# Routing and expert loop of a hybrid decoder layer: expert 0 first and loaded during routing, down projection one block behind, its weights on GpSimd's queue

## The chip, the cores and the metric

The kernel runs on one core of a Trainium2 chip. The metric is device time in microseconds for one launch of the whole layer; the median of several runs is compared.

## The reference, cut to what matters

One decoder layer over 2048 tokens of width 1024: a parallel pair of attention and state-space heads, an output projection, and then a mixture of experts with 32 experts in 4 groups. Each token goes to the two best experts of its best group. The part that this change touches:

```
g_sel = argmax(h @ w_router_group + b)                 # 1 of 4 groups
top_p, top_i = top_k(softmax(e_logits of that group), 2)
dest: rows sorted by expert, each expert padded to whole blocks of 128 rows
for each block of 128 rows, with its expert e:
    hid = silu(xb @ w_gate[e]) * (xb @ w_up[e])        # 1024 -> 512
    out = hid @ w_down[e]                              # 512 -> 1024
x = x + sum over a token's two rows of gate * out row
```

All inputs and outputs are float32. w_gate, w_up and w_down take 2 MiB for each expert, 6 MiB in all.

## The kernel before, in words

The layer is a chain of stages, each a function with its own semaphores and one or more blocks in which the five engines run their own programs. A stage ends with a barrier over all engines. The three last stages matter here: `route`, `experts`, `combine`.

`route` (lines 1238 to 1404) is one long chain of small VectorE instructions, almost each waiting for the one before it. It finds the two experts of each token, counts rows with two TensorE matmuls (`pref_done`), sums the counts in 16 additions into `rank_base` (line 1365), compares them with block edges (1367), reduces to blocks for each expert (1369), makes a prefix sum (1370) and a difference (1371), and writes the tables `slot_ids` (the 128 token numbers of each block) and `block_meta` (for each block the place of its expert among the experts that have rows; then their numbers, and the count of blocks and experts). ScalarE computes three exponentials here, GpSimd prepares a few constants at the start, and SyncE has nothing to do.

`experts` (lines 1407 to 1620) has two blocks. The first only sets buffers and semaphores (VectorE memsets) and stores one block of zeros. In the second each engine loops over the filled blocks of 128 rows, of which there are 49 for this input; the number is known only at run time.

- SyncE loads gate, up and down weights of expert after expert, each 2 MiB in one transfer into one buffer (`w_gate_raw` and so on). It waits until the earlier expert's weights in that buffer have been split.
- Every float32 matmul is done in three passes over values split into a high part (float32r) and a low part. ScalarE makes the high part of weights by a copy (`split_hi`, line 1488), VectorE the low part by subtraction (`split_lo`, line 1533), each in halves of 128x2048. The split weights have one buffer only, so a new expert's weights can be split only when TensorE has finished with the old ones. All splits stand under a test that the next block's expert differs (`where_below`).
- GpSimd gathers the rows of the next block with an indirect DMA, after TensorE has transposed the rows of the block before.
- TensorE does for block b: gate (24 matmuls, line 1576 on), up (24), the first half of the transposes of the rows of block b+1 (`rows_T(0)`, line 1569), the transposes of the hidden values (line 1603), `rows_T(1)`, and down (24 matmuls, lines 1614 to 1619).

The hidden values of block b are `silu(gate) * up`. So between the last up matmul and the transposes stands a VectorE multiplication (line 1551), and between the transposes and the first down matmul a ScalarE copy (line 1510):

```
                    product(U, 1, u_done)
                    pe.wait_ge(x_in, 16 * b + 32)
                    rows_T(0)
                    pe.wait_ge(hid_done, b + 2)
                    ...
                    rows_T(1)
                    pe.wait_ge(hh_done, b + 2)
```

`combine` gathers each token's two result rows, adds them and makes the final norm. It isn't touched.

## Time and profile before

| | us |
|---|---|
| median of 3 runs | 2601.83 |
| lowest and highest | 2600.53, 2602.84 |
| the profiled execution's own time | 2598.93 |
| its span in the profile | 2597.2 |
| `route`, about | 1464.8 to 1508 |
| `experts`, up to TensorE's first weight matmul | 1509.3 to 1542.6 |
| `experts`, block loop, about | 1542.6 to 2502 |
| `combine`, about | 2506 to 2597 |

Times within the profile are microseconds from the start of the span. PE is TensorE, PEld its weight loads, DVE is VectorE, ACT is ScalarE, POOL is GpSimd, SP is SyncE. A TensorE matmul's duration in the rows reaches over the start of the next one, so the distance between two starts is the better measure of its cost.

### The profile page before, as it was taken

The numbers are of one execution on the slowest core, as the hardware profiler recorded it, in microseconds if no ns is written. First come the engines' busy times: TensorE is split into PE (matmuls) and PEld (weight loads), VectorE is DVE, ScalarE is ACT, GpSimd is POOL, SyncE is SP. The second block draws the span as 40 slices with busy tenths as digits, with TensorE's granted clock in tenths as the row PEclk, the third lists the DMA queues.
The fourth block names the chain that finished last, engine by engine and source line by source line (L and its number), as shares of the span: only waits on it lengthen the run. The fifth ranks groups of instructions, "written<-read, shape, count | busy, mean of one in ns | idle before, by whom it ended". The sixth has DMA issues, their size and how long they took to land. (4 is left out here: it accounts for less than half of the span.)

```text
span 2597.2 us, 29608 instructions
## 1 busy us (share of the span) xinstructions
PE 2193.0 (84%) x9806; PEld 1650.3 (64%) x9807; DVE 1421.5 (55%) x2441; ACT 1110.1 (43%) x1586; POOL 276.6 (11%) x348
## 2 busy tenths in 40 slices
PE   4999999948969687876999549999999999999950
PEld 3764444448447576765888437777777777777740
DVE  4831582045258576674544557566648847354548
ACT  6101111012317576665222126566647847355432
POOL 0002331024220110000000000000000000000022
PEclk6999999979869898998999759999999999999985
DMA  7023443172742514311433158477758958454649
GB/s 223 33 73 138 170 142 118 41 245 112 314 112 69 114 27 88 86 29 51 134 128 134 51 218 347 186 282 279 279 210 340 370 227 333 168 198 195 253 172 378
DMA packets 128019, 458.76 MB, mean 177 GB/s; under 512 B 25136, under 2 KB 41536, under 8 KB 113600
## 3 DMA queue, kind: packets, MB, share of 16 engines
q1 hardware_dynamic: 98352, 345.22, 38.0%
q0 software_dynamic: 18928, 69.49, 7.1%
q10 hardware_dynamic: 10656, 43.00, 4.0%
q8 instruction: 46, 0.75, 0.1%
q14 instruction: 37, 0.30, 0.0%
HBM read 342.06 MB, written 115.61 MB: 176 GB/s over the span
## 5 line engine op out<-in xcount | busy, mean ns | idle before, releaser
L1533 DVE TENSOR_TENSOR w_gate_lo<-w_gate_raw,w_gate_hi 128x2048 fp32r<-128x2048 f32 x64 | 146.3, 2286 | 179.0 <-ACT w_gate_hi L1488 179.0
L895 DVE CUSTOM_DVE_ANT_0 scores<-c_bank,alibi 128x512 f32<-128x512 f32 (+3 forms) x320 | 175.4, 607 | 109.0 <-PE c_bank L993 108.8
L488 PE MATMUL a_bank<-w_in_chunk,hT 128*128 128x512 f32 x512 | 221.9, 596 | 0.7 <-ACT hT L266 0.7
L488 PE MATMUL a_bank<-hT,w_in_chunk 128*128 128x512 f32 x512 | 220.6, 593 | 0.0
L300 ACT ACTIVATE proj_out<-a_bank 128x512 f32<-128x512 f32 x64 | 38.2, 597 | 398.7 <-PE a_bank L488 389.4
L488 PEld LDWEIGHTS a_bank<-w_in_chunk,hT 128*128 128x128 f32 x512 | 128.8, 252 | 92.7 <-issue 62.6
L1007 PE MATMUL c_bank<-v_head,map_T 128*128 128x128 f32 x1088 | 152.2, 289 | 41.7 <-ACT map_T L951 41.7
L1576 PE MATMUL m_bank<-w_gate_hi,rows_T_hi 128*128 128x512 f32 x392 | 154.9, 395 | 24.2 <-DVE rows_T_lo L1537 24.2
L1614 PE MATMUL m_bank<-w_down_hi,hidden_T_hi 128*128 128x512 f32 x392 | 160.4, 409 | 16.2 <-ACT hidden_T_hi L1510 16.2
L488 PEld LDWEIGHTS a_bank<-hT,w_in_chunk 128*128 128x128 f32 x512 | 97.0, 190 | 120.9 <-issue 120.8
L1007 PEld LDWEIGHTS c_bank<-v_head,map_T 128*128 128x128 f32 x1088 | 136.2, 198 | 57.4 <-ACT map_T L951 57.4
L992 PE MATMUL c_bank<-k_hi,q_parts 128*128 128x512 f32 (+3 forms) x320 | 126.9, 401 | 43.9 <-DMA k_lo<-kT_d 37.8
L940 ACT ACTIVATE scores<-scores,neg_max 128x128 f32<-128x128 f32 (+15 forms) x128 | 152.6, 1199 | 19.6 <-DVE neg_max L900 19.5
L1578 PE MATMUL m_bank<-w_gate_hi,rows_T_lo 128*128 128x512 f32 x392 | 157.1, 401 | 0.0
L1578 PE MATMUL m_bank<-w_up_hi,rows_T_lo 128*128 128x512 f32 x392 | 156.1, 398 | 0.0
L1577 PE MATMUL m_bank<-w_gate_lo,rows_T_hi 128*128 128x512 f32 x392 | 155.4, 397 | 0.0
L1615 PE MATMUL m_bank<-w_down_lo,hidden_T_hi 128*128 128x512 f32 x392 | 155.2, 396 | 0.0
L1577 PE MATMUL m_bank<-w_up_lo,rows_T_hi 128*128 128x512 f32 x392 | 154.5, 394 | 0.0
L1576 PE MATMUL m_bank<-w_up_hi,rows_T_hi 128*128 128x512 f32 x392 | 153.8, 392 | 0.0
L1533 DVE TENSOR_TENSOR w_up_lo<-w_up_raw,w_up_hi 128x2048 fp32r<-128x2048 f32 x64 | 143.5, 2283 | 1.7 <-ACT w_up_hi L1488 1.7
L1488 ACT ACTIVATE w_gate_hi<-w_gate_raw 128x2048 fp32r<-128x2048 f32 x64 | 122.3, 1912 | 51.5 <-DMA w_gate_raw<-in_w_gate_dram 51.1
L1533 DVE TENSOR_TENSOR w_down_lo<-w_down_raw,w_down_hi 128x2048 fp32r<-128x2048 f32 x64 | 143.4, 2282 | 0.4 <-ACT w_down_hi L1488 0.4
(375 smaller groups left out, 4427.0 us busy)
## 6 DMA issues: line engine op xcount, KB each, us to landing
w_gate_raw<-in_w_gate_dram SPq DMA_DIRECT2D x32, 2048.0 KB, 7.8
w_up_raw<-in_w_up_dram SPq DMA_DIRECT2D x32, 2048.0 KB, 10.7
w_down_raw<-in_w_down_dram SPq DMA_DIRECT2D x32, 2048.0 KB, 10.7
rows_d<-rows_out ACTq DMA_DIRECT2D x50, 512.0 KB, 10.3
rows_d<-zero_rows POOLq DMA_DIRECT2D x34, 512.0 KB, 18.6
x_tile<-in_x_dram SPq DMA_DIRECT2D x16, 512.0 KB, 3.8
w_in_chunk<-in_w_in_dram POOLq DMA_DIRECT2D x4, 2048.0 KB, 14.9
qT_d<-xn_tile SPq DMA_DIRECT2D x32, 256.0 KB, 3.1
```

The costliest lines, as they stand in the source:

```text
L488: last = pe.matmul(bank[4 + n % PB][:], lhsT, rhs, start=kt == 0, stop=kt == KT - 1)
L895: dve.tensor_tensor_reduce(S[:, s, m, c * BANK:c * BANK + w], bank[n % 4][:, 0:w], bias[:, h % 2, x0:x0 + w], 1.0, -BIG, ALU.add, ALU.max, ...
L940: act.activation(S[:, s, m, 0:L], S[:, s, m, 0:L], ACT.Exp, bias=nm[:, s, m:m + 1], accum_out=rs[:, s, m:m + 1]).then_inc(exped, 1)
L992: pe.matmul(bank[n % 4][:, 0:w], qt, kh[:, m, cols].bitcast(F32R), start=True, stop=False)
L1007: last = pe.matmul(bank[6 + u % 2][:, 0:VD], aT[:, n % 2, b * P:(b + 1) * P], v[:, h % 2, kt], start=kt == 0, stop=kt == u % NT)
L1488: act.activation(whi[w][:, s], raw[w][:, s], ACT.Copy).then_inc(hi_done[w], 1)
L1533: dve.tensor_tensor(wlo[w][:, s], raw[w][:, s], whi[w][:, s], ALU.subtract).then_inc(lo_done[w], 1)
L1576: pe.matmul(to[:], xh[:, k], whi[w][:, c], start=k == 0, stop=False)
L1577: pe.matmul(to[:], xh[:, k], wlo[w][:, c], start=False, stop=False)
L1578: last = pe.matmul(to[:], xl[:, k], whi[w][:, c], start=False, stop=k == KT - 1)
L1614: pe.matmul(DN[h][:], hh[:, k], whi[2][:, part(k)], start=k == 0, stop=False)
L1615: pe.matmul(DN[h][:], hh[:, k], wlo[2][:, part(k)], start=False, stop=False)
```

## The change

In `route`: the weight buffers and their semaphores are made before the stage (class `ExpertStore`). SyncE starts the loads of expert 0's gate and up weights at the start of the stage, GpSimd those of its down weights. ScalarE splits off all six high halves. The low halves: VectorE makes the first of gate, in its chain after the gates are computed and ahead of the wait for `pref_done`; GpSimd makes the second of gate and both of up; the two of down are made by VectorE at the start of `experts`. Expert 0 gets at least one block, so that it is always first. GpSimd makes the zero block and sets three semaphores, ScalarE stores the zeros. The first block of `experts` goes away.

In `experts`: the loop runs over blocks but one. TensorE's order in iteration j is gate of block j+1, transposes of the hidden values of block j, up of block j+1, both halves of the row transposes of block j+2, down of block j. Loads are in halves of 1 MiB, each issued when its half of the buffer has been split; the down halves are issued by GpSimd after its gather. ScalarE copies out both halves of the result, of which VectorE made one before, and loads the table with Silu once before the loop.

```
-def route(nc, ident, ones, logits, gates, dest, ids, meta, d):
+def route(nc, ident, ones, logits, gates, dest, ids, meta, store, a, d):
...
+            def split_lo(eng, w, i):
+                eng.wait_ge(hi_done[w], i + 1)
+                return eng.tensor_tensor(wlo[w][:, halves[i]], raw[w][:, halves[i]], whi[w][:, halves[i]], ALU.subtract)
+
+            @block.sync
+            def _(sp):
+                for w in range(2):
+                    for i in range(2):
+                        sp.dma_start(raw[w][:, halves[i]], store.source(a, w, slice(0, 1), i)).then_inc(w_in[w][i], 16)
...
+                for i in range(2):
+                    pool.dma_start(raw[2][:, halves[i]], store.source(a, 2, slice(0, 1), i)).then_inc(w_in[2][i], 16)
+                pool.memset(store.out[:], 0.0).then_inc(primed, 1)
...
+                pool.wait_ge(lo_done[0], 1)
+                split_lo(pool, 0, 1).then_inc(lo_done[0], 1)
+                split_lo(pool, 1, 0).then_inc(lo_done[1], 1)
+                split_lo(pool, 1, 1).then_inc(lo_done[1], 1)
...
                 act.activation(gex[:], gex[:], ACT.Exp).then_inc(exp_done, 1)
+                act.wait_ge(primed, 1)
+                act.dma_start(d["rows"][NBLK], store.out[:]).then_inc(store.out_st, 16)
+                split_hi(0, 0)
                 act.wait_ge(exp_in, 3)
...
+                split_hi(0, 1)
+                for w in range(1, 3):
+                    for i in range(2):
+                        split_hi(w, i)
+                act.wait_ge(store.out_st, 16)
...
+                split_lo(dve, 0, 0).then_inc(lo_done[0], 1)
                 dve.wait_ge(pref_done, 1)
...
+                step(dve.tensor_scalar(nblk[:, 0:1], nblk[:, 0:1], 1.0, None, ALU.max))
...
+                step(dve.tensor_scalar(bf[0:1, META_LATER:META], pend[0:1, NE - 1:NE], -1.0, None, ALU.add))
...
 (experts, SyncE)
+                with sp.Fori(1, n) as o:
+                    e = expert(sp, o)
+                    for w in range(2):
+                        for i in range(2):
+                            sp.wait_ge(lo_done[w], 2 * o - 1 + i)
+                            load(sp, w, e, i)
 (GpSimd)
+                with pool.Fori(2, n) as b:
+                    past, now = place(pool, b - 2), place(pool, b - 1)
+                    e = expert(pool, now + 1)
+                    pool.wait_ge(xT_psum, 2 * b + 2)
+                    gather(b + 1)
+                    with where_below(nc, pool, past, now):
+                        for i in range(2):
+                            pool.wait_ge(lo_done[2], 2 * now + 1 + i)
+                            load(pool, 2, e, i)
 (ScalarE)
+                act.preload_act_table(ACT.Silu)
...
+                with act.Fori(0, later(act)) as j:
+                    before, now, order = place(act, j), place(act, j + 1), place(act, j + 2)
+                    hidden_hi(j + 1)
+                    act.wait_ge(g_done, j + 2)
+                    act.wait_ge(hid_done, j + 1)
                     act.activation(sil[:], G[:], ACT.Silu).then_inc(silu_done, 1)
                     with where_below(nc, act, now, order):
+                        split_hi(0, order, 0)
+                        split_hi(0, order, 1)
+                    rows_hi(0, 2 * j + 5)
+                    rows_hi(1, 2 * j + 6)
                     with where_below(nc, act, now, order):
+                        act.wait_ge(u_done, j + 2)
+                        split_hi(1, order, 0)
+                    out_half(0, j)
                     with where_below(nc, act, now, order):
+                        split_hi(1, order, 1)
+                    out_half(1, j)
+                    store(j)
+                    with where_below(nc, act, before, now):
+                        split_hi(2, now, 0)
+                        split_hi(2, now, 1)
 (VectorE)
+                with dve.Fori(0, later(dve)) as j:
+                    before, now, order = place(dve, j), place(dve, j + 1), place(dve, j + 2)
+                    hidden_lo(j + 2)
                     with where_below(nc, dve, now, order):
+                        split_lo(0, order, 0)
+                        split_lo(0, order, 1)
+                    hidden(j + 1)
+                    rows_lo(0, 2 * j + 5)
+                    rows_lo(1, 2 * j + 6)
                     with where_below(nc, dve, now, order):
+                        split_lo(1, order, 0)
+                        split_lo(1, order, 1)
+                    with where_below(nc, dve, before, now):
+                        split_lo(2, now, 0)
+                        split_lo(2, now, 1)
 (TensorE: gate and up of block 0 and the row transposes of block 1 stand ahead of the loop)
+                with pe.Fori(0, later(pe)) as j:
+                    before, order = place(pe, j), place(pe, j + 1)
...
+                    product(G, 0, g_done)
+                    hidden_T(j)
...
+                    product(U, 1, u_done)
+                    pe.wait_ge(x_in, 16 * j + 48)
+                    rows_T(0)
+                    rows_T(1)
+                    down(j, before)
+                end = later(pe)
+                hidden_T(end)
+                down(end, place(pe, end))
```

`store.source(a, w, e, i)` is the half i of weight w of expert e in memory, laid out as before. `down` waits for both down halves (`hi_done[2]`, `lo_done[2]`) and for `d_used`, both copies of the result before.

## Rows read from the trace of the kernel before

**Rows 1.** The page's head, and its part on DMA issues.

```profile
span 2597.2 us, 29608 instructions
...
w_gate_raw<-in_w_gate_dram SPq DMA_DIRECT2D x32, 2048.0 KB, 7.8
...
w_in_chunk<-in_w_in_dram POOLq DMA_DIRECT2D x4, 2048.0 KB, 14.9
```

**Rows 2.** Windows view: busy us of each engine (instructions), granted clock, DMA share, GB/s.

```profile
1510.50:1542.50 32.00, 1.97 (x8) 1.57 (x8) 14.68 (x8) 12.10 (x8) 2.62 (x5) 0.50 0.93 372
1542.50:2500.00 957.50, 918.12 (x4109) 738.18 (x4110) 568.52 (x430) 576.01 (x511) 64.60 (x144) 1.00 0.65 252
1563.10:1621.60 58.50, 56.11 (x253) 45.12 (x253) 44.71 (x31) 40.47 (x35) 4.04 (x9) 1.00 0.95 370
2537.00:2547.00 10.00, 0.00 (x0) 0.00 (x0) 9.29 (x12) 2.48 (x6) 4.10 (x4) 0.50 1.03 417
```

**Rows 3.** Waits in the block loop: us in total, times, longest.

```profile
ACT w_gate_hi L1488 <- DMA w_gate_raw<-in_w_gate_dram: 2.1, 1, 2.1
PE m_bank L1603 <- DVE hidden L1551: 22.6, 48, 2.3
PE m_bank L1614 <- ACT hidden_T_hi L1510: 15.8, 47, 0.5
```

**Rows 4.** Timeline of one block in the loop, TensorE: start, us, what.

```profile
2001.63 0.40 PE L1576 MATMUL m_bank<-w_up_hi,rows_T_hi 128*128 128x512 f32 x1
...
2007.24 0.60 PE L1569 MATMUL m_bank<-ident,rows_in 128*128 128x128 f32 x4
...
2008.27 0.75 PE L1603 MATMUL m_bank<-ident,hidden 128*128 128x128 f32 x4 [0.43 <-DVE hidden L1551]
...
2008.85 0.61 PE L1569 MATMUL m_bank<-ident,rows_in 128*128 128x128 f32 x4
...
2009.85 0.50 PE L1614 MATMUL m_bank<-w_down_hi,hidden_T_hi 128*128 128x512 f32 x1 [0.39 <-ACT hidden_T_hi L1510]
...
2015.55 0.39 PE L1576 MATMUL m_bank<-w_gate_hi,rows_T_hi 128*128 128x512 f32 x1
```

**Rows 5.** Timeline of the start of the expert stage, all engines.

```profile
1509.29 0.91 DVE L1444 MEMSET rows_out<- 128x1024 f32 x1 [1.24 <-PEq L62]
...
1511.06 0.18 POOL L1473 COPY idx<-slot_ids 128x1 int32<-128x1 int32 x1 [44.88 <-POOLq L1440]
...
1516.43 1.97 PE L1569 MATMUL m_bank<-ident,rows_in 128*128 128x128 f32 x8 [9.33 <-DMA rows_in<-h_d,idx]
...
1523.48 3.71 ACT L1488 ACTIVATE w_gate_hi<-w_gate_raw 128x2048 fp32r<-128x2048 f32 x2 [49.05 <-DMA w_gate_raw<-in_w_gate_dram]
1525.43 4.49 DVE L1533 TENSOR_TENSOR w_gate_lo<-w_gate_raw,w_gate_hi 128x2048 fp32r<-128x2048 f32 x2 [15.01 <-ACT w_gate_hi L1488]
...
1540.89 1.28 DVE L1537 TENSOR_TENSOR rows_T_lo<-m_bank,rows_T_hi 128x512 fp32r<-128x512 f32 x2
...
1542.63 0.76 PE L1576 MATMUL m_bank<-w_gate_hi,rows_T_hi 128*128 128x512 f32 x1 [24.22 <-DVE rows_T_lo L1537]
```

**Rows 6.** Timeline of VectorE within the routing.

```profile
1479.93 0.09 DVE L1363 MEMSET rank_base<- 128x32 f32 x1 [2.74 <-PE r_bank L1301]
...
1483.59 0.69 DVE L1367 TENSOR_TENSOR compare<-rank_base,block_edges 128x512 f32<-128x512 f32 x1
```

**Rows 7.** Timeline of an earlier stage: VectorE beside GpSimd, and alone.

```profile
558.12 1.25 POOL L552 TENSOR_TENSOR sin_z<-z_state,table_batch 128x510 f32<-128x510 f32 x1
558.35 1.57 DVE L573 TENSOR_TENSOR z_in<-z_in,z_tmp 128x512 f32<-128x512 f32 x1
...
565.53 0.69 DVE L573 TENSOR_TENSOR z_in<-z_in,z_tmp 128x512 f32<-128x512 f32 x1
```

**Rows 8.** Groups by line in the block loop, ScalarE: busy us, mean ns.

```profile
L1505 ACT ACT_TABLE_LOAD x49 | 62.9, 1283 | 37.4 <-issue 36.9
...
L1505 ACT ACTIVATE silu<-m_bank 128x512 f32<-128x512 f32 x49 | 29.4, 600 | 1.3 <-PE m_bank L1578 0.8
```

More of the change, by code:

```diff
@@ L1460, in _, with load @@
+            def load(eng, w, e, i):
+                eng.dma_start(raw[w][:, halves[i]], store.source(a, w, bass.ds(e, 1), i)).then_inc(w_in[w][i], 16)
             @block.sync
@@ L1496, in _, with store @@
+                def store(b):
+                    act.wait_ge(d_used, 2 * b + 4)
+                    act.dma_start(d["rows"][bass.ds(b, 1)].rearrange("o p n -> p (o n)"), out[:]).then_inc(out_st, 16)
+                act.preload_act_table(ACT.Silu)
                 rows_hi(0, 1)
                 rows_hi(1, 2)
-                with act.Fori(0, blocks(act)) as b:
-                    now, order = place(act, b), place(act, b + 1)
-                    with where_below(nc, act, now, order):
-                        act.wait_ge(g_done, b + 1)
-                        split_hi(0, order, (0,))
-                    act.wait_ge(g_done, b + 1)
-                    act.wait_ge(hid_done, b + 1)
+                first, second = place(act, 0), place(act, 1)
@@ L1542, in _ @@
+                split_lo(2, 0, 0)
                 rows_lo(0, 1)
                 rows_lo(1, 2)
[L1544 to L1563 removed]
@@ L1565, in _ @@
+                end = later(dve)
+                hidden_lo(end + 2)
             @block.tensor
```

254 lines of the change are left out of this document (136 added, 118 removed).

## The prediction, made before the changed kernel was run

> **What bounds the kernel now.** I read the page first [rows 1], then the windows view, to see which engine fills each stretch [rows 2]. In the block loop TensorE is busy 918.1 of 957.5 us at the full clock of 2.4 GHz (1.00), while VectorE has 568.5, ScalarE 576.0 and the DMA engines a share of 0.65. So TensorE sets the loop, and all that can be won there is its idle time, 39.4 us, plus what its pipeline loses in refilling after each wait. Ahead of the loop stands the opposite: 32 us in which TensorE does 2 us of work and the DMA engines are 0.93 busy. These 32 us are a load, not arithmetic.
>
> The waits view says what the loop's 39.4 us are [rows 3]: 22.6 us before the transposes of the hidden values, for the VectorE product, and 15.8 us before down, for the ScalarE copy, both about once in every block. The timeline of one block shows them in place [rows 4]: up from 2001.63 to 2007.24, transposes, 0.43 idle, hidden transposes, row transposes, 0.39 idle, down from 2009.85, next gate at 2015.55. The block takes 5.60 (gate, 2015.55 to the next up by the same 24 matmuls) + 5.61 + 2.61 + 5.70, that is 19.5. Up's 24 matmuls take 5.61 and down's 5.70, so a restart costs some 0.1 beyond the idle time shown.
>
> The start of the expert stage [rows 5] shows that the gather index is read at 1511.06, rows are there at 1516.43, but the first weights only at 1523.48, and that splitting the three weights one after the other (ScalarE 3.71, VectorE 4.49 each pair) puts the low part of the rows, queued behind them on VectorE, at 1540.89 and the first matmul at 1542.63.
>
> **Part 1: what `route` takes on.** Loads: 6.29 MB at the 417 GB/s that a full stretch reached [rows 2] take 15 us; from 1465 they end by about 1483. ScalarE's halves of 1.86 each [rows 5] follow and end by about 1488; its exponentials are waited for once, at about 1476, ahead of which only one half stands, loaded first. Cost 0 to 2 us if that half is late; I take 0. VectorE's own low half (4.49 / 2 = 2.25) stands in front of the wait for the counts, where VectorE idled 2.74 [rows 6]: 0, and 2.25 if that wait were shorter. Two added one-value or 32-value instructions of VectorE: about 0.2 each, 0.4 us.
>
> The three low halves on GpSimd are the doubtful part. No GpSimd subtraction of 128x2048 is in the trace. A 128x510 one took 1.25 [rows 7]; four times that is 5.0, and scaled as VectorE's do (0.69 for 512 [rows 7], 2.25 for 2048 [rows 5]) it is 4.1. I take 4.6, so 14 us from about 1479.6 on, done long before the stage's end at 1508. But rows 7 also show that they aren't free for VectorE: its L573, with both inputs in SBUF, takes 0.69 alone and 1.57 when it starts 0.23 after a GpSimd multiplication of 1.25. It ended at 559.92, that is 0.55 after GpSimd's end: it stood still until GpSimd had finished. In `route` VectorE's 16 additions read PSUM and one SBUF tile, and I let them run. Then come, from 1483.59 [rows 6], instructions with two SBUF inputs. Compare stands until GpSimd's first half ends at 84.2: 0.6 lost. During compare's 0.69 GpSimd's second half stands and then runs 84.9 to 89.5. VectorE does the reduction and the maximum, about 0.9, and stands at the prefix sum until 89.5: 3.7 lost. The third half slips in behind it, 89.7 to 94.3, and the difference stands 4.6 less a little. Together 8.7 us (7.3 to 10 with halves of 4.1 to 5.0; 0 if the additions or luck keep the two apart). `route` gets longer by 8.7 + 0.4 = 9.1.
>
> The Trainium skill has this as a rule (SBUF — State Buffer, Who interferes with whom): an exclusive lock, held for a whole instruction, between a GpSimd instruction that reads SBUF and a VectorE one with two SBUF inputs. The trace agrees (1.57 against 0.69). With that rule the route costs the 9.1 above; without it 0.4, which is the second rival.
>
> **Part 2: the start of `experts`.** The first block goes: index at 1511.06 came 1.77 after the point 1509.29 at which the stage's first instruction can start [rows 5]; −1.8. From the index the rows need 5.37 as before, then 1.97 for eight transposes at the lower clock, and 0.6 + 0.65 + 0.45 for high part, low part and TensorE's start, about 9.0, since gate's and up's splits are done and only one half of down (2.25) stands ahead on VectorE while the rows are on their way. Before it was 1542.63 − 1511.06 = 31.6. Gain 22.5. Parts 1 and 2 together: −15.2.
>
> **Part 3: the loop.** In the new order each TensorE step has work between it and what it needs, so I take both waits and the restarts as gone: 39.4 + 48 x 0.1 = 44.2. What covers them, counted from the end of a gate, in a block after which the expert changes (TensorE: hidden transposes to 0.6, up to 6.2, row transposes to 7.4, down to 13.0, gate to 18.6):
> - ScalarE: hidden copy to 1.3, Silu to 1.9, two gate halves to 5.7, two row copies (0.6 each, as Silu [rows 8]) from 7.0 to 8.2, up half to 10.1, result half to 10.9, up half to 12.8, result half to 13.7, store, two down halves to 18.0. It needs six halves and six copies, 15.1 of 18.6.
> - VectorE: hidden low to 2.0, gate lows to 8.4, product to 9.1, row lows to 10.4, up lows to 15.2, down lows to 20.7, ahead of 26.0 where down wants them. It needs 13.5 + 2.7 = 16.2 of 18.6.
> - Next gate at 13.0 wants row lows (10.4) and gate lows (8.4); next up at 19.2 wants 15.2. Nothing is late; the tightest has 2.6 us.
> - Loads: each half of 1 MiB is asked for when its low half is done (6.1 to 20.7) and wanted 14 us later. SyncE has four of them in a block. GpSimd issues the down halves after its gather, and nothing else is queued behind them but the next gather, wanted 5 us later still. If the cover goes, a late load costs its lateness.
>
> The table load of 1.283 ahead of each Silu [rows 8] ought to go, as Silu's table is loaded ahead of the loop and the copies are found under it. If one stays in each block ScalarE needs 16.4, if two 17.7, still below 18.6. The Trainium skill puts the price of a change of table at 1283 ns plus 1380 ns of drain (ScalarE: Activation LUTs, What ACT_TABLE_LOAD costs). The row has the first number. By the sum with drain two loads would make 20.4 and ScalarE the bound; the trace shows no such second part in the block loop, where Silu follows its load directly.
>
> New costs: the first switch has no filled pipeline. Block 0's gate ends 8 us after the first matmul (slow clock for about 5 of it, as before). From there Silu and two gate halves take ScalarE to 12.4, VectorE's lows, product and row lows end at 17.2, and TensorE, free at 14.7, stands 2.5. If its clock falls to 1.2 GHz in that gap, as it stood in the load stretch (0.50 [rows 2]), a microsecond more: 3.5. The last block still has one wait for its hidden copy, 0.9. Loop: −44.2 + 3.5 + 0.9 = −39.8. The weights' semaphores now end with a clearing and barrier of their own behind the stage; the like at the stage's start left VectorE idle 1.24, of which a part is other work: +0.8.
>
> **Sum.** −15.2 − 39.8 + 0.8 = −54.2 us. The profiled execution had 2598.93 (span 2597.2), so 2544.7; the median of the runs is 2.9 above it, so 2547.6, and I say 2547. `combine` is bound by the DMA engines (1.03 busy [rows 2]) and stays.
>
> **The rivals.**
> - *No standing still in `route`* (0.12): the lock falls between VectorE's instructions, or hits only those with time. 8.7 less: 2538 or 2539. For it: VectorE's instructions are short. Against: rows 7.
> - *The loop gets a new bound, the transfers* (0.18). An expert's block moves 6.29 MB of weights and 1.05 of rows, 7.34 MB. In three such blocks in a row the DMA engines were 0.95 busy at 370 GB/s [rows 2]. That would be 389 at 1.0, or 18.9 us against TensorE's 18.6; at 370 it is 19.8. Over the 31 changes that is 9 to 37 us before the 14 us of cover are spent, so I say half, 20: 2567. Against: 417 GB/s in another stretch, and one wait of 2.1 us for weights in all of the loop [rows 3].
> - *The waits don't go but move* (0.07): TensorE's new waits, or an engine's order, take as much as the two removed. Only −15.2 + 3.5 + 0.8 remain: about 2591. Against: the 2.6 us of room above.
> - *Slower: down weights late on GpSimd's queue* (0.08). Before, GpSimd's own loads took 14.9 us for 2 MiB against 7.8 on SyncE's [rows 1]. A down half is wanted 14 us after its issue and down itself has 5 us more. If a half took over 19 us to land, TensorE would stand at each of 31 changes; from 21 us on that eats the 54 us (1.75 each), and at 25 us it makes 31 x 6 = 186 and about 2735. Against: 14.9 was for twice the bytes.
>
> **How the numbers follow.** The forecast has 0.55; its own range, from the ends of the GpSimd halves, 2 us for a late exponential and 0.1 to 0.2 us left in each block, is 2541 to 2556. The range of all reaches down to the first rival and up beyond the second: 2535 to 2572, which leaves out the last two rivals and the second's worse half, under 2 in 10. A measurement here can tell 0.2%, 5 us. Faster 0.91, same 0.01, slower 0.08.
>
> **What the changed profile would show.** First weight matmul about 15 us earlier, at 1527; in `route` two or three VectorE instructions of 0.2 to 0.7 us drawn out to 4 or 5 beside GpSimd's three subtractions; no waits at the hidden transposes and down; starts of successive gates 18.6 apart, whether the expert changes or not; no table load in the loop; one gap of 2.5 us before the second gate. I'd be wrong if gates lay over 19 apart in runs of changes with ScalarE waiting for weights, or if VectorE's chain in `route` kept its length.

## The result, and the profile after

The changed kernel takes 2531.64 us (median of 4 runs, 2527.51 to 2532.77) against 2602.18 us for the kernel before, run beside it (2600.53 to 2602.84). The ratio is 0.9727, with an interval of 0.971 to 0.9744: 70.5 us faster. The forecast was 54 us faster, and 2531.6 lies 3.4 us below the low end of the range, 2535. The profiled execution had 2532.77, with a span of 2531.1 us, against 2597.2 [rows 1]: 66.1 us less. The changed kernel's profiled execution is the longest of its four, and that of the kernel before lay 3.3 us under its median. So the traces account for 66.1 of the 70.5 us, and the other 4.4 are spread between executions of one kernel.

The page's head and its part on DMA issues:

```profile
span 2531.1 us, 30844 instructions
...
w_gate_raw<-in_w_gate_dram SPq DMA_DIRECT2D x64, 1024.0 KB, 6.8
...
w_down_raw<-in_w_down_dram POOLq DMA_DIRECT2D x64, 1024.0 KB, 6.7
```

Weights now come in halves of 1 MiB. The halves on GpSimd's queue land in 6.7 us at the median, no later than those on SyncE's.

The span splits at three marks. When `route` starts, the trace after lies 0.7 us behind that of before (its first VectorE instruction is at 1464.25 and not 1463.53). The change touches nothing ahead of that, so the first line of the table would be −10.1 without this drift.

| Mark, us | before | after | change |
|---|---|---|---|
| start of the span to the first weight matmul | 1542.6 | 1533.2 | −9.4 |
| first weight matmul to the end of the last one | 959.4 | 902.3 | −57.1 |
| from there to the end of the span | 95.2 | 95.6 | +0.4 |

The sum is −66.1, the difference of the two spans. The forecast for the same three was −15.2, −39.8 and +0.8.

**The loop.** Windows view, with columns as in [rows 2]: the whole block loop, two blocks in a row that both change the expert, and the last block.

```profile
1533.00:2436.00 903.00, 892.20 (x4116) 735.52 (x4116) 544.98 (x384) 504.04 (x480) 122.31 (x207) 0.99 0.70 268
1924.00:1960.20 36.20, 36.20 (x169) 29.88 (x168) 31.93 (x21) 28.63 (x24) 6.38 (x10) 1.00 0.97 373
2416.00:2436.00 20.00, 11.99 (x42) 9.20 (x40) 5.09 (x3) 6.45 (x7) 0.00 (x0) 0.74 0.07 27
```

TensorE stands for 10.8 us of the loop where it stood for 39.4 [rows 2]. The second row is the one to read for the blocks: 36.20 busy of 36.20. Two blocks fit into it, so one is 18.1 us. The timeline of TensorE in one of them:

```profile
1942.11 1.04 PE L1663 MATMUL m_bank<-ident,rows_in 128*128 128x128 f32 x8
1942.90 0.48 PE L1691 MATMUL m_bank<-w_down_hi,hidden_T_hi 128*128 128x512 f32 x1
...
1948.56 0.39 PE L1670 MATMUL m_bank<-w_gate_hi,rows_T_hi 128*128 128x512 f32 x1
...
1954.15 0.63 PE L1680 MATMUL m_bank<-ident,hidden 128*128 128x128 f32 x4
1954.54 0.48 PE L1670 MATMUL m_bank<-w_up_hi,rows_T_hi 128*128 128x512 f32 x1
...
1960.20 1.04 PE L1663 MATMUL m_bank<-ident,rows_in 128*128 128x128 f32 x8
```

Start to start: row transposes 0.79, down 5.66, gate 5.59, hidden transposes 0.39, up 5.66, together 18.09. In [rows 4] the block took 19.52, of which the same three kinds of weight matmuls had 16.9 and everything between the last up and the first down 2.61. That 2.61 has become 0.79 + 0.39 = 1.18. So this block got 1.43 us shorter, though the waits of [rows 4] showed only 0.43 + 0.39 = 0.82. By the starts of the gates in the whole trace of before, the blocks after which the expert changes (31 of 49) took 19.52 and the other 18 took 19.37, with a second wait of 0.24 in place of 0.39; the mean is 19.46. Now all take 18.09 or 18.10.

All waits of TensorE for a semaphore in the loop are now these (us in total, times, longest):

```profile
PE m_bank L1691 <- DVE w_down_lo L1610: 7.5, 1, 7.5
...
PE m_bank L1670 <- issue: 2.6, 1, 2.6
PE m_bank L1670 <- ACT rows_T_hi L1545: 1.5, 1, 1.5
```

Each stands there once: the last block's down, block 0's second gate, and the very first weight matmul. Nothing waits for weights in between. On ScalarE no table load is left in the loop. Before there were 80: the 49 ahead of Silu [rows 8], and 31 more of 1283 ns at line 1488, ahead of the first half of a new gate's split, which [rows 8] leave out. The timeline at the last block's down:

```profile
2419.00 0.63 PE L1680 MATMUL m_bank<-ident,hidden 128*128 128x128 f32 x4
2427.14 0.79 PE L1691 MATMUL m_bank<-w_down_hi,hidden_T_hi 128*128 128x512 f32 x1 [7.51 <-DVE w_down_lo L1610]
2427.73 0.63 PE L1692 MATMUL m_bank<-w_down_lo,hidden_T_hi 128*128 128x512 f32 x1
2428.16 0.63 PE L1691 MATMUL m_bank<-w_down_hi,hidden_T_hi 128*128 128x512 f32 x1
...
2432.79 0.39 PE L1692 MATMUL m_bank<-w_down_lo,hidden_T_hi 128*128 128x512 f32 x1
2433.01 0.39 PE L1691 MATMUL m_bank<-w_down_hi,hidden_T_hi 128*128 128x512 f32 x1
```

After standing 7.5 us, TensorE runs twelve matmuls at 0.43 apart and then goes back to 0.23: the granted clock fell from its upper to its lower level (0.50 from 2429 to 2432; 0.74 is the mean over the window of 20 us). The twelve take 5.3 us, from 2427.14 to the second half's first start at 2432.43; at the upper level twelve take 2.8 (twelve of the 24 that take 5.6 in the loop), so the clock costs 2.5 us here.

**`route`.** Timeline of VectorE and GpSimd:

```profile
1480.33 4.51 POOL L1279 TENSOR_TENSOR w_gate_lo<-w_gate_raw,w_gate_hi 128x2048 fp32r<-128x2048 f32 x1 [11.22 <-DVE w_gate_lo L1279]
...
1484.33 1.07 DVE L1404 TENSOR_TENSOR compare<-rank_base,block_edges 128x512 f32<-128x512 f32 x1
1484.82 9.41 POOL L1279 TENSOR_TENSOR w_up_lo<-w_up_raw,w_up_hi 128x2048 fp32r<-128x2048 f32 x2
...
1486.34 3.52 DVE L1408 TENSOR_TENSOR_SCAN block_end<-ones,n_blocks 128x32 f32<-128x32 f32 x1
1489.90 4.38 DVE L1409 TENSOR_TENSOR slot_base<-block_end,n_blocks 128x32 f32<-128x32 f32 x1
```

Compare takes 1.07 and not 0.69 [rows 6]; the prefix sum and the difference, 0.22 and 0.19 before, take 3.52 and 4.38. The difference ends at 1494.28, and GpSimd's last half at 1494.23. The prefix sum ends 3.52 after its start, at 1489.86, somewhat behind the end of the half before. VectorE's reduction between them isn't drawn out, and neither are the 16 additions with one input in PSUM, all of them beside GpSimd's first half: 3.51 us against 3.50 before.

**The start of `experts`.** Timeline, from the gather's index on:

```profile
1518.02 0.19 POOL L1509 COPY idx<-slot_ids 128x1 int32<-128x1 int32 x1 [23.79 <-POOLq L62]
1518.04 2.31 DVE L1610 TENSOR_TENSOR w_down_lo<-w_down_raw,w_down_hi 128x2048 fp32r<-128x2048 f32 x1 [1.01 <-PEq L62]
1518.29 2.11 POOL L1511 TENSOR_TENSOR hold<-ones 128x1 f32<-128x1 f32 x1
1519.83 0.90 SPq L1494 DMA_DIRECT2D w_gate_raw<-in_w_gate_dram  x2
1520.57 1.05 POOL L1512 DMA_INDIRECT rows_in<-h_d,idx  x1 [0.16 <-issue]
1520.83 1.07 SPq L1494 DMA_DIRECT2D w_up_raw<-in_w_up_dram  x2
1529.76 1.97 PE L1663 MATMUL m_bank<-ident,rows_in 128*128 128x128 f32 x8 [13.85 <-DMA rows_in<-h_d,idx]
...
1533.19 0.77 PE L1670 MATMUL m_bank<-w_gate_hi,rows_T_hi 128*128 128x512 f32 x1 [1.46 <-ACT rows_T_hi L1545]
```

The index is read 6.96 us later than before, 6.3 without the drift. From it to the first weight matmul 15.2 us pass (31.6 before, 9.0 forecast). Two things stand in between: the one-value addition `hold`, 2.11 instead of 0.19, beside VectorE's subtraction that began 0.25 us ahead of it; and a gather that needs 9.2 us from its issue to the transposes, with 4 MiB of the next expert's weights asked for around it. Before, the gather was issued at 1511.83, and SyncE's first request came at 1513.53, behind it; now the first comes 0.74 ahead.

### The profile page after: what moved, and what is told of

The parts are those of the page before. It is cut to its first block and busy times, and to the rows that moved or that the text cites. A ratio compares the mean times of both kernels' runs of the same rounds, so it can differ in the third digit from the quotient of the medians.

```text
span 2531.1 us, 30844 instructions
## 1 busy us (share of the span) xinstructions
PE 2164.5 (86%) x9806; PEld 1645.6 (65%) x9807; DVE 1395.1 (55%) x2378; ACT 1039.1 (41%) x1556; POOL 353.3 (14%) x421
## 5 line engine op out<-in xcount | busy, mean ns | idle before, releaser
L1610 DVE TENSOR_TENSOR w_gate_lo<-w_gate_raw,w_gate_hi 128x2048 fp32r<-128x2048 f32 x62 | 139.3, 2288 | 32.0 <-ACT w_gate_hi L1541 32.0
L1610 DVE TENSOR_TENSOR w_up_lo<-w_up_raw,w_up_hi 128x2048 fp32r<-128x2048 f32 x62 | 141.6, 2285 | 10.8 <-ACT w_up_hi L1541 10.8
L1541 ACT ACTIVATE w_down_hi<-w_down_raw 128x2048 fp32r<-128x2048 f32 x62 | 115.3, 1907 | 20.9 <-ACT rows_out L1555 20.9
```

What stands on the lines that cost most here:

```text
L1541: act.activation(whi[w][:, halves[i]], raw[w][:, halves[i]], ACT.Copy).then_inc(hi_done[w], 1)
L1610: dve.tensor_tensor(wlo[w][:, halves[i]], raw[w][:, halves[i]], whi[w][:, halves[i]], ALU.subtract).then_inc(lo_done[w], 1)
```

## The experiments

Each ratio is to the kernel before, run beside the experiment on the same chip; that kernel's medians were 2600.8 to 2602.4 us. The changed kernel's own four times spread over 5.3 us, so differences to it of under some 5 us are read from the traces and not from the times. A trace's clock has to be set back first: `route`, whose start no experiment touches, begins at 1460.0 to 1465.0 us in these traces. Each diff is cut to the edit's core. Those that start with b edit the kernel before, those with a the changed kernel, and o1 joins the two.

**b1 and b2: the waits taken out of the old order.** How much does a block get shorter in the kernel before if only the waits go? b2 transposes a constant tile in place of the product:

```diff
-                    pe.wait_ge(hid_done, b + 2)
...
-HT[:, k * P:(k + 1) * P], hid[:, k:FF:FT], ident[:])
+HT[:, k * P:(k + 1) * P], still[:, k:FF:FT], ident[:])
```

b1 also lets down read constant parts, so that the second wait goes too:

```diff
-                    pe.wait_ge(hh_done, b + 2)
...
-                        if h == 0:
-                            pe.wait_ge(hl_done, b + 2)
-pe.matmul(DN[h][:], hh[:, k], whi
+pe.matmul(DN[h][:], still_h[:, k], whi
```

> The kernel before, with its order of work, but TensorE transposes a constant tile in place of the hidden values and uses constant high and low parts in down; the product, the copies and everything else still run. This leaves out the dependence of down on the hidden values and nothing of the work. Theory A (each wait and each short group of transposes costs more than the idle time shown, because the ends of matmuls are modelled): blocks 18.1 to 18.2 apart in place of 19.5, 1.35 us x 48 = 65 less, 2537 to 2542. Rival B (the waits cost what is shown, 39.4 us and 0.1 for each restart, as in the prediction; the rest comes from the new order of transposes): blocks 18.6 apart, about 2558. Either could be held back by late weights, since gate's are wanted 8.5 us after their request in this order: then ScalarE waits for w_gate_raw.

> The kernel before, with only the first of the two waits taken away: TensorE transposes a constant tile in place of the hidden values; down still waits for the ScalarE copy of those transposes. Theory A (a wait costs some 0.25 us beyond the idle time shown): 22.6 + 12 = 35 less, 2567. Rival B (only the idle time shown and 0.1 for the restart): 22.6 + 5 = 27 less, 2575. If the second wait simply takes over the first one's time: 2595 or more.

b1 took 2555.5 us (2549.41 to 2558.16), ratio 0.9819 [0.9793, 0.9846], some 47 us faster. Timeline of TensorE in a block after which the expert changes:

```profile
2085.56 0.60 PE L1575 MATMUL m_bank<-ident,rows_in 128*128 128x128 f32 x4
2085.99 0.65 PE L1608 MATMUL m_bank<-ident,still 128*128 128x128 f32 x4
2086.48 0.61 PE L1575 MATMUL m_bank<-ident,rows_in 128*128 128x128 f32 x4
2086.84 0.48 PE L1618 MATMUL m_bank<-w_down_hi,still_T_hi 128*128 128x512 f32 x1
...
2103.74 0.60 PE L1575 MATMUL m_bank<-ident,rows_in 128*128 128x128 f32 x4
```

This decides how long the waits were. With the order of the steps unchanged, the block falls from 19.52 to 18.18 (one without a change of expert from 19.37 to 18.18), and the stretch from the last up to the first down from 2.61 to 1.28: 1.33 us of true waiting, where the profile showed 0.82. The reason can be read in the second column. Four transposes carry a duration of 0.60 to 0.65, but the next group starts 0.43, 0.49 and 0.36 after them. A matmul's duration holds its passage through a pipeline in which the next one already runs. Ahead of a wait that tail is counted as work, though nothing is behind it. Two waits in a block hide 2 x 0.25 us. (Without a change of expert the row shows 0.67 and the starts give 1.19, the same 0.5 hidden.)

The whole kernel fell short of some 63 us (31 x 1.34 + 18 x 1.19), because the old order stands on something else as soon as two or more blocks in a row change the expert: the requests for gate's weights lie 19.2 to 21.9 us apart in such runs. Around a single change the blocks take 18.2. Its waits in the loop:

```profile
ACT rows_out L1522 <- DMA rows_d<-rows_out: 35.6, 12, 5.2
PE m_bank L1582 <- DVE w_gate_lo L1539: 19.1, 12, 3.4
```

b2 took 2583.76 us (2577.71 to 2594.52), ratio 0.9943 [0.9919, 0.9967], 15 us faster, and neither theory's number came out. The third guess, that the second wait takes over the first one's time, holds for the blocks with a change alone. Blocks without a change of expert went from 19.37 to 18.68, those with one stayed at 19.52. Its waits view says why:

```profile
PE m_bank L1619 <- ACT hidden_T_hi L1516: 41.1, 49, 3.2
```

This wait was 15.8 [rows 3]. Freed of the first wait, TensorE arrives at the second earlier and stands there, 1.09 us in place of 0.39, in each block after which the expert changes. In the others the second wait keeps its 0.24. The two have to go together.

**o1: the new start with the old loop.** It has everything of the change in `route` and at the stage's start, and the loop of the kernel before:

```diff
# against the kernel before, beside the changed route()
-                with sp.Fori(0, n) as o:
+                with sp.Fori(1, n) as o:
...
-                for w in range(3):
-                    split_lo(w, 3)
+                split_lo(2, 1)
```

> The new routing with expert 0 loaded and split in it, and the block loop as it was (2 MiB loads on SyncE, VectorE copying out the second half of the result, table loads in the loop, 49 rounds in the old order); down's loads in the routing are issued by SyncE. What the start alone is worth. By the timelines of both kernels the first weight matmul comes 9.4 us earlier (1533.2 against 1542.6) and the end has one barrier more, 0.6: about 2593. By the prediction's part on the start, 15.2 less 0.8: 2588. The difference to the changed kernel, about 61, is then the loop alone; had the loop given 39.8, as predicted, it would be 2571.

2588.43 us (2578.11 to 2594.38), ratio 0.9955 [0.9937, 0.9973]: the start is worth about 12 us by the medians (7 to 16 by the interval), and the changed kernel is 57 us faster than that, which is what its loop gained by the marks above. By its trace the first weight matmul comes 7.8 us nearer to the start of `route` than before, against 10.2 in the changed kernel: o1's first gather takes 13.0 us from its issue to the transposes, with whole loads of 2 MiB asked for around it. And its loop, to the end of the last matmul, takes the 959 us of before. The two waits are there as before: 24.6 us for the product and 16.8 for the ScalarE copy, in 49 each (22.6 and 15.8 [rows 3]).

**a1: the low halves back on VectorE**, at the start of `experts`, in place of GpSimd's in `route`:

```diff
-                split_lo(pool, 0, 1).then_inc(lo_done[0], 1)
-                split_lo(pool, 1, 0).then_inc(lo_done[1], 1)
-                split_lo(pool, 1, 1).then_inc(lo_done[1], 1)
...
+                split_lo(0, 0, 1)
+                split_lo(1, 0, 0)
+                split_lo(1, 0, 1)
                 split_lo(2, 0, 0)
                 rows_lo(0, 1)
```

> The changed kernel, with the three low halves of GpSimd in the routing moved to VectorE at the start of the expert stage, ahead of its first half of down. If the lock between GpSimd and VectorE costs what the timeline shows (0.4 + 3.3 + 4.2 = 7.9 us in three instructions of VectorE), and the 6.9 us of added splits lie in the 11.2 us that VectorE waits for the gathered rows: 7.9 less, about 2524. If the three drawn-out instructions are slow for another reason, the routing keeps its length and the time stays at 2531. If the start is bound by VectorE after all: 2524 + 7 = 2531 with a short routing.

2525.73 us (2523.19 to 2526.32), ratio 0.9709 [0.9686, 0.9731]. The first weight matmul starts at 1526.12, 7.1 us earlier than in the changed kernel or, counted from the start of `route`, 6.5, and the span is 6.6 shorter. VectorE has the time for all four halves while the rows are on their way, and `route` has its 7.9 us back; 1.5 of them are lost again between the stage's start and the first weight matmul. So GpSimd's three halves cost what they were said to cost, and bought nothing that VectorE had no time for. The same lock shows from the other side here (timeline):

```profile
1509.49 2.31 DVE L1606 TENSOR_TENSOR w_gate_lo<-w_gate_raw,w_gate_hi 128x2048 fp32r<-128x2048 f32 x1 [1.01 <-PEq L62]
1509.75 2.11 POOL L1507 TENSOR_TENSOR hold<-ones 128x1 f32<-128x1 f32 x1
1511.73 4.48 DVE L1606 TENSOR_TENSOR w_up_lo<-w_up_raw,w_up_hi 128x2048 fp32r<-128x2048 f32 x2
1512.02 2.90 POOL L1508 DMA_INDIRECT rows_in<-h_d,idx  x1 [0.16 <-issue]
```

GpSimd's `hold` and then its gather's issue (1.05 in the changed kernel) stand beside VectorE's subtractions. The issue is 1.85 us longer, which covers the 1.5 lost.

**a2: GpSimd's halves later in `route`**, beside the one-hot comparisons, which have one tensor input:

```diff
                 pool.wait_ge(lo_done[0], 1)
+                pool.wait_ge(slots_ready, 2)
                 split_lo(pool, 0, 1)
```

> The changed kernel, with GpSimd's three low halves held back until VectorE has made its first one-hot table, so that they run beside 64 small VectorE instructions that read one SBUF tensor each. If the two engines stand in each other's way only where VectorE reads two tensors of SBUF: compare, prefix sum and difference are back at 0.7 and 0.2 us, only the product ahead of the second batch of one-hots is drawn out, by 2 to 4.5 us, and the time is 4 to 6 us less than the changed kernel's 2531, about 2526. If any VectorE instruction on SBUF stands while GpSimd works, the one-hots stretch by up to 13.5 us and the time is 2531 to 2537.

2534.93 us (2524.61 to 2537.19), ratio 0.975 [0.9705, 0.9794]; the span is 2532.2. My guess that these would pass undisturbed fell:

```profile
1488.58 0.28 DVE L1430 TENSOR_SCALAR slot_row_onehot<-count,slot_place 128x128 fp32r<-128x128 f32 x1
...
1488.78 4.58 DVE L1431 TENSOR_SCALAR slot_block_token<-count,slot_place,token_id 128x64 fp32r<-128x64 f32 x1
1488.81 4.49 POOL L1279 TENSOR_TENSOR w_gate_lo<-w_gate_raw,w_gate_hi 128x2048 fp32r<-128x2048 f32 x1 [23.29 <-DVE slot_block_token L1431]
1493.27 8.94 POOL L1279 TENSOR_TENSOR w_up_lo<-w_up_raw,w_up_hi 128x2048 fp32r<-128x2048 f32 x2
1493.28 4.57 DVE L1430 TENSOR_SCALAR slot_row_onehot<-count,slot_place 128x128 fp32r<-128x128 f32 x1
```

Comparisons of 0.28 us take 4.5 to 4.6 beside a GpSimd half, three in a row, about 12.8 us in all. Compare, prefix sum and difference are back at 0.69, 0.23 and 0.19. The standing still moved with GpSimd's work.

**a3: the first gather ahead of the loads.** SyncE waits for the rows before it asks for the next expert:

```diff
+                sp.wait_ge(x_in, 16)
                 with sp.Fori(1, n) as o:
```

> The changed kernel, with SyncE's loads for the second expert held back until the first rows have been gathered. If the first gather lands late (9.2 us from its issue against 4.6 before) because four loads of 1 MiB were issued 0.7 us ahead of it: it lands in about 4.6 us again, the first weight matmul comes 4.5 us earlier, the loads still come in time for the second gate, and the time is about 2527. If the gather is slow for another reason: 2531 to 2533. If the held-back loads are then late for the second gate's split, part of it is lost again there.

2528.06 us (2524.96 to 2529.7), ratio 0.9728 [0.969, 0.9767]; the span is 2528.1, 3.0 shorter. Timeline:

```profile
1521.32 1.04 POOL L1513 DMA_INDIRECT rows_in<-h_d,idx  x1 [0.16 <-issue]
1525.88 1.97 PE L1664 MATMUL m_bank<-ident,rows_in 128*128 128x128 f32 x8 [9.21 <-DMA rows_in<-h_d,idx]
```

From issue to transposes 4.56 us instead of 9.19, so the first weight matmul comes 4.6 us nearer to the start of `route`. The loads start 7 us later and are still early enough: the second gate stands the same 2.60 us. The times alone would not show it (2524.96 to 2529.7 against 2527.51 to 2532.77).

Here and in a1 and a9 the traces show a cost that the changed kernel's doesn't have. After the same 2.6 us without work, the second gate's matmuls fell to the lower clock for a while. Timeline of a9:

```profile
1533.11 0.47 PE L1671 MATMUL m_bank<-w_gate_hi,rows_T_hi 128*128 128x512 f32 x1 [2.60 <-issue]
...
1534.88 0.63 PE L1671 MATMUL m_bank<-w_gate_hi,rows_T_hi 128*128 128x512 f32 x1
1535.30 0.63 PE L1672 MATMUL m_bank<-w_gate_lo,rows_T_hi 128*128 128x512 f32 x1
```

The granted clock is 0.50 from 1536 to 1537, and the gate takes 7.22 us (7.21 in a3, 7.22 in a1) in place of 5.66 in the changed kernel, a6, a10 and a11. No run here shows what decides between the two. The 1.6 us are part of why the spans of a1 and a3 gained less than their starts.

**a5 and a10: down's weights on SyncE's queue.** Does the second queue matter? In a5 SyncE asks, for each expert, for gate, up and down in this order; a10 keeps all on SyncE but asks for gate and up of the next expert ahead of down of the one before (in both, GpSimd's own loads of down are taken out, too):

```diff
# a5
-                    for w in range(2):
+                    for w in range(3):
                         for i in range(2):
                             sp.wait_ge(lo_done[w], 2 * o - 1 + i)
                             load(sp, w, e, i)
# a10, behind gate and up of o + 1
+                    for i in range(2):
+                        sp.wait_ge(lo_done[2], 2 * o - 1 + i)
+                        load(sp, 2, late, i)
```

> The changed kernel, with all of down's loads on SyncE's queue in place of GpSimd's, behind those of gate and up. In the changed kernel TensorE waits for no load in the loop, and down's halves are wanted 14 us after their request and more: the queue makes no difference, 2529 to 2534. If GpSimd's queue is what keeps SyncE's loads on time (two queues side by side), blocks 18.1 apart become longer in runs of new experts: 5 to 20 us more, with ScalarE waiting for weights.

> As a5, all of down's loads on SyncE's queue, but issued in the order in which their buffers come free: gate and up of expert o+1, then down of expert o. In a5 SyncE waited for down's low halves of the expert before and behind that wait stood the next expert's gate, whose buffer had been free for one block's length. If that order of waits was what cost 85 us, and not the queue's hardware: 2529 to 2534 again, blocks 18.09 apart. If one hardware queue is too slow for all weights: 2545 and more, ScalarE waiting for weights in runs of new experts.

a5 took 2616.2 us (2607.73 to 2621.81), ratio 1.0066 [1.0046, 1.0087]: 85 us slower than the changed kernel, and slower than the one before. Both theories had expected far less. The waits of a5 in the loop:

```profile
ACT w_gate_hi L1525 <- DMA w_gate_raw<-in_w_gate_dram: 88.8, 18, 9.7
...
PE m_bank L1654 <- issue: 67.4, 10, 8.2
```

and those of SyncE's own instruction stream:

```profile
SPq L1492 <- DVE w_down_lo L1594: 661.6, 61, 21.6
```

In the new order down's low parts are made one block later than gate's and up's. SyncE stands at down's semaphore while gate's buffer is already free, and gate's load starts late. a10 took 2530.26 us (2526.74 to 2532.21), ratio 0.9724 [0.9708, 0.974], the same as the changed kernel. So it isn't the queue that GpSimd's loads go through which is worth the 85 us, but that no load is asked for behind a wait that ends later than its own.

**a6: without the preload of Silu's table.**

```diff
-                act.preload_act_table(ACT.Silu)
```

> The changed kernel without the load of Silu's table ahead of the loop. The trace will then have one or two table loads of 1.28 us in each round of the loop. ScalarE needs 15.1 us of the 18.09 of a block after which the expert changes; with one load 16.4, with two 17.7, and its register loads come on top. If the slack in ScalarE's schedule takes them: 2531 to 2533. If ScalarE becomes the bound in runs of new experts (a block over 18.09 with TensorE waiting for row copies or down's splits): 5 to 25 us more.

2528.69 us (2521.03 to 2532.01), ratio 0.9727 [0.9685, 0.9769]. From the stage's start to its end there is one table load of 1283 ns, at the first Silu, and none in the loop.

The preload is not what removed the 80 loads. o1, with the new `route` and the old loop, has them all again (49 and 31), so it is the new loop that removed them. In it the first Silu stands ahead of the loop, which is then entered with Silu's table in any case; that this is the reason is my reading, and no run here tests it.

**a11: gate's and up's halves asked for together**, so that a load has the size of before:

```diff
                     for w in range(2):
+                        sp.wait_ge(lo_done[w], 2 * o)
                         for i in range(2):
-                            sp.wait_ge(lo_done[w], 2 * o - 1 + i)
                             load(sp, w, e, i)
```

> The changed kernel, with gate's and up's halves requested together, when both halves of the buffer are split, as the kernel before did. The first half is then asked for 2.3 us later, of 14 us of cover. If the loop keeps its 18.09 because the new order leaves 12 to 14 us between request and use, in place of 8.5 before: 2530 to 2533. If requesting by halves is what keeps the loads on time: blocks of over 18.5 in runs of new experts and 5 us more or above.

2528.65 us (2527.25 to 2531.29), ratio 0.9719 [0.9705, 0.9734]: no difference. Asking in halves gives nothing here; the 12 to 14 us between a free buffer and its next use cover a whole load.

**a9: all of it together.** a1 and a3, the first gather without its `hold`, and the last down begun as soon as the first half of its weights is split:

```diff
-                gather(0)
+                gather(0, held=False)
...
-down(end, place(pe, end))
+down(end, place(pe, end), halfway=True)
```

> The changed kernel with the costs that its trace shows at the start and the end taken out together: the three low halves on VectorE at the start of the expert stage (a1, 6.6 us of span), the second expert's loads behind the first gather (a3, 3.0), the first gather without the small GpSimd addition in front, which stood 2.1 us against VectorE's split (1.9), and the last down begun when the first halves of its weights are split instead of both (it stood 7.5 us for them; about 2 and some of the slow clock back). If these are separate costs they add up: 13 us less than the changed kernel, about 2518. If the start is then bound by VectorE, whose four splits of 2.28 and the wait for the gather lie side by side (9.2 against 5 to 6 us), some 3 of it are not there: 2521. Then the low part of the rows comes after the splits and not after the gather.

2518.81 us (2514.96 to 2522.19), ratio 0.9681 [0.9667, 0.9696], 12.8 below the changed kernel. The first weight matmul starts at 1516.23, 17.0 us earlier than there, but `route` starts 4.1 us earlier, too (1460.13 against 1464.25), with which the change has nothing to do: 12.8 are left. The last block's timeline:

```profile
2409.22 0.79 PE L1698 MATMUL m_bank<-w_down_hi,hidden_T_hi 128*128 128x512 f32 x1 [5.36 <-DVE w_down_lo L1608]
```

5.4 us of standing instead of 7.5. From the hidden transposes to the end of the last matmul it is 14.9 us in place of 16.5, so 1.6 are won there, and the 1.6 for the lower clock in the second gate (a3) take them away again. The profiled execution's span is 2514.0 against 2531.1, and 4.1 of these 17.1 us are the earlier start of `route`; the other 13 are what the medians say and what was expected.

## Why the prediction was right and where it failed

**`route`, +9.1: right.** The three drawn-out instructions are the ones named, at the places named, and cost 0.4 + 3.3 + 4.2 = 7.9 where 8.7 was said; by the first comparison behind them the chain is 8.1 us longer. A GpSimd half takes 4.5 (4.6 said), so the bound by VectorE's scaling was the nearer. VectorE's own half in front of the wait was hidden: 0.42 of the 2.74 idle was left. The rival without the lock is refuted by these rows, and a1 gives the price as a time, some 6 us. The rule of the Trainium skill (SBUF — State Buffer, Who interferes with whom) holds for the three: the VectorE instructions with two SBUF inputs stood until GpSimd's instruction was over. That comparisons with one SBUF tensor and a value per partition stand as well I read from a2 alone.

**The start, −24.3: the mechanism right, some 6 us too much.** The step that failed is "from the index the rows need 5.37 as before". Before, the gather was issued 1.7 us ahead of the first load. The prediction noted that gate's and up's splits are done by then, but not that SyncE may therefore ask for the next expert at once, ahead of the gather. a3 puts the cost at 4.6 us (9.19 against 4.56). GpSimd's `hold`, taken at 0.2, stood 1.9 in the lock. The prediction applied the lock in one direction only, to VectorE's instructions in `route`, and not to GpSimd's beside the half of down that it had itself placed there. Together they are 6.5 us, against 6.2 too much (15.2 from the index to the first weight matmul where 9.0 was said).

**The loop, −39.8 against −57.1: the failed step is the term 39.4 + 48 x 0.1 = 44.2.** The two waits went, as said, and no new one took their place in the blocks. But the term was made of the idle time that the waits view shows. b1, which changes nothing but the waits, shows 1.33 us for each block with a change and not 0.92, and the changed kernel's hidden transposes take 0.1 less than b1's (0.39 against 0.48). Over all blocks the loop got 70.3 us shorter by this and not 44.2: 49 x (19.46 − 18.09) = 67.3, and 3.0 for the one block before that stood for weights (22.53 in place of 19.52). The forecast of 18.6 for a block has the same mistake: it took transposes at the durations shown, 0.6 for a group of four, where a group costs 0.4. Could it have been seen in advance? Yes: the starts of two up matmuls are 0.23 apart (24 of them take 5.61 in [rows 4]) and the duration of each is 0.39 to 0.40. An end that is modelled 0.16 after the next start says that every idle time behind it is shown too short. The text above the prediction itself calls the distance between starts the better measure, and the sum didn't use it.

**The last block: a term that was missing.** The prediction gave 0.9 to the last wait. It counted that down's low parts end 5 us ahead of their use in the loop, where a gate and an up stand between one block's down and the next one's. In the last block, which also changed the expert, there is only the group of hidden transposes: down's buffer of split weights comes free at 2419.0, when the down before has ended, ScalarE copies out a half of the result and splits from 2420.47 on, VectorE's second half ends at 2426.9, and TensorE starts at 2427.14. By the starts that is 7.75 us of standing, and the lower clock behind it costs 2.5, together 10.2.

The sum of the loop then goes: −67.3 for the blocks, −3.0 for the one stall of before, +2.85 before the second gate, +7.75 and +2.5 in the last block. That makes −57.2, and 57.1 was measured. For the second gate 3.5 was said, 2.5 for the gap and 1 for the clock; in this trace the clock stayed up (the matmuls behind the gap are 0.23 apart), in a1, a3 and a9 it fell and cost 1.6. In the prediction's terms, 26.1 us too little were taken from the loop and 8.7 too little put to it. That the two traces' difference, 66.1, lies only 12 us from the forecast of 54.2 owes something to luck: the 5.8 us that the start fell short and these 8.7 both stood against the 26.1.

**The last microseconds.** The traces are 66.1 us apart; taken off the 2601.8 from which the prediction started that is 2535.7, at the very edge of its range. The rest down to 2531.6 is spread between executions. The range itself was also narrower than it says: what it leaves out is 0.07 + 0.08 and the worse half of 0.18, 0.24 and not under 2 in 10.

**The end, +0.8: about right.** From `last_copy` to SyncE's next issue 1.63 us pass instead of 1.05, +0.6.

**The transfers as the bound: refuted, but closely.** Blocks in a row with a change take 18.09, as those without, with TensorE without a gap, at a DMA share of 0.97 and 373 GB/s. The second of the two has 0.99 and 401 GB/s, which is 7.25 MB, near the 7.34 counted. By my estimate from that share, little more could be taken off a block before the transfers bound it in such runs. **The waits that move: refuted** for this order, though b1 and b2 show it as what happens in the old one. **Slower by down's queue: refuted** with 6.7 us for a half, where more than 19 would have been needed. a5 shows that a change close to this one does end on the slower side, by a mechanism that no rival named: a load behind another load's wait on the same engine.

Open stays how the loads slow the gather. Its issue takes 1.05 us in the changed kernel and 1.04 in a3, so they slow what comes behind it, but where isn't told apart. Open is also what brings the lower clock after the 2.6 us of standing in some runs and not in others. That the last block's 10.2 us would go if the last expert had a second block, so that down's split weights were there in time, wasn't tried.

## What to carry to other kernels

A wait's idle time in the profile is what is left after the modelled end of the instruction before it. On a pipelined engine measure a wait by starts: the distance from the last start before it to the first start after it, less what the same steps need back to back. Use that for the gain. Before work is given to an engine that is free, look at what its neighbour does in the same microseconds: a long GpSimd subtraction held short VectorE instructions for its whole length here, and the other way round, though not reductions and not additions with one input in PSUM. And when a producer's steps are moved against each other, move the loads' waits with them: the order of waits on the issuing engine was worth 85 us here, the choice of the queue nothing.

## What the runs showed that was not expected

- A VectorE comparison of 128x64 or 128x128 with one SBUF tensor and one or two values per partition took 4.50 to 4.58 us beside a GpSimd subtraction of 4.49, and 0.28 to 0.31 alone (a2). A reduction of 128x512 beside such a subtraction took its 0.69 as ever.
- GpSimd stands too: beside VectorE's subtractions a one-value addition took 2.11 instead of 0.19 (a1, the changed kernel), and the issue of a gather 2.90 (a1), 2.52 (o1) or 2.48 (a9) instead of 1.05.
- A gather of 0.5 MB took 9.2 us from its issue to its use with 4 MiB of loads asked for ahead of and around it, and 4.6 alone (the changed kernel, a3). It took 4.6 as well with 6 MiB asked for from 1.7 us behind it (the kernel before).
- After 7.5 us without work TensorE ran twelve matmuls at its lower clock (the changed kernel). After 2.6 us it ran none in the changed kernel, a6, a10 and a11, but seven or eight in a1, a3 and a9, at a cost of 1.6 us.
- The first table load in a round of the old loop stood ahead of a copy and not of Silu, in each of the 31 blocks after which the expert changes. The prediction took the copies as found under Silu's table, and the new loop bears it out: copies and Silu run there without a load.
